# The convolution's running sums in PSUM, and the gate stage's low weight parts on GpSimd

## The reference

```python
h = rmsnorm(x, ln_pre[i])
z = h @ w_in[i]
(c_val, c_glu, c_gate, q, k, v, a_gate, g_conv, g_attn) = split_columns(z)
ya = conformer_conv(c_val, c_glu, w_dw[i], b_dw[i], conv_ln_g[i], conv_ln_b[i], w_pw[i])
ya = (ya * jax.nn.silu(c_gate)) @ w_br_conv[i]
yb = sliding_window_sink_attention(q, k, v, sinks[i], positions)
yb = (yb * jax.nn.silu(a_gate)) @ w_br_attn[i]
m = jax.nn.sigmoid(g_conv) * ya + jax.nn.sigmoid(g_attn) * yb
x = x + rmsnorm(m @ w_out[i], ln_post[i])
x = x + jax.nn.sigmoid(x @ w_ple_gate[i]) * (p[i] @ w_ple_proj[i])
```

## Time and profile before

| | |
|---|---|
| median of 3 runs | 1147.31 us (1146.74 to 1150.53) |
| the profiled execution | 1147.26 us, of which the span from the first to the last instruction is 1145.5 us |
| TensorE busy | 1139.3 us, 99% of the span, 6208 matmuls |
| VectorE busy | 925.0 us, 81%, 1087 instructions |
| ScalarE busy | 421.8 us, 37% |
| GpSimd busy | 29.8 us, 3%, 32 instructions |
| low parts on VectorE (line 1561) | 96 of 1224 ns mean, 117.5 us |
| taps on VectorE (line 1738) | 232, 300.1 us |
| share of TensorE in the chain that ended last | 92% |

### The profile page before, as it was taken

How to read it: one execution, slowest core, us unless ns; L and a number is a source line. 1 busy time by engine, 2 the same in 40 slices (tenths; PEclk the granted TensorE clock), 3 DMA queues, 4 the chain that set the end, 5 groups by cost and what they waited for, 6 DMA issues and landing times.

```text
span 1145.5 us, 16085 instructions
## 1 busy us (share of the span) xinstructions
PE 1139.3 (99%) x6208; PEld 927.8 (81%) x6208; DVE 925.0 (81%) x1087; ACT 421.8 (37%) x763; POOL 29.8 (3%) x32
## 2 busy tenths in 40 slices
PE   9999999999999999999999999999999999999998
PEld 7788888888888888877777788888888888888887
DVE  5999999999999977489888589768767967557776
ACT  6422212212112121266666343332536435444342
POOL 2012010000000000000000000000000000000000
PEclk9999999999999999999999999999999999999999
DMA  9726787421221322411111211346553753334565
GB/s 350 286 92 179 206 238 201 111 92 55 73 86 50 111 51 65 101 38 57 57 57 57 74 49 44 92 135 205 166 173 120 252 182 127 115 117 141 182 200 184
DMA packets 46053, 148.00 MB, mean 129 GB/s; under 512 B 5648, under 2 KB 6416, under 8 KB 43952
## 3 DMA queue, kind: packets, MB, share of 16 engines
q1 hardware_dynamic: 32176, 92.77, 25.5%
q10 hardware_dynamic: 11520, 37.75, 9.5%
q0 software_dynamic: 2304, 16.78, 6.1%
HBM read 119.37 MB, written 41.94 MB: 141 GB/s over the span
## 4 chain that ended last, share of the span: by engine, by line
PE 92%; DMA 3%; DVE 3%; ACT 1%; SPq 1%; issue 1%; DVEq 0%; ACTq 0%
PE psg L629 66%; PE psb L1013 10%; PE psg L921 6%; DMA conv<-xT 2%; PE psb L835 1%; PE psg L892 1%; PE psg L1013 1%; PE psg L682 1%; PE psg L966 1%; PE psg L853 1%; ACT probs L1237 1%; PE psg L887 1%; PE psg L653 1%; PE psg L1037 1%; SPq L496 0%
## 5 line engine op out<-in xcount | busy, mean ns | idle before, releaser
L629 PE MATMUL psg<-h_hi,w_hi 128*128 128x512 f32 x768 | 236.8, 390 | 0.0
L629 PE MATMUL psg<-h_lo,w_hi 128*128 128x512 f32 x768 | 236.5, 389 | 0.0
L629 PE MATMUL psg<-h_hi,w_lo 128*128 128x512 f32 x768 | 236.4, 389 | 0.0
L1561 DVE TENSOR_TENSOR w_lo<-w_raw,w_hi 128x1024 fp32r<-128x1024 f32 x96 | 117.5, 1224 | 86.9 <-ACT w_hi L1093 83.4
L629 PEld LDWEIGHTS psg<-h_hi,w_hi 128*128 128x128 f32 x768 | 143.8, 188 | 30.5 <-issue 0.8
L629 PEld LDWEIGHTS psg<-h_lo,w_hi 128*128 128x128 f32 x768 | 144.1, 188 | 30.0
L629 PEld LDWEIGHTS psg<-h_hi,w_lo 128*128 128x128 f32 x768 | 144.1, 188 | 29.9
L1738 DVE SCALAR_TENSOR_TENSOR conv<-u,cols,conv 128x1024 f32<-128x1024 f32 x120 | 154.3, 1286 | 0.0
L1738 DVE SCALAR_TENSOR_TENSOR work<-u,cols,work 128x1024 f32<-128x1024 f32 x112 | 145.8, 1301 | 0.0
L1093 ACT ACTIVATE w_hi<-w_raw 128x1024 fp32r<-128x1024 f32 x95 | 100.5, 1057 | 103.8 <-PE psg L629 86.4
L1013 PE MATMUL psb<-s_hi,pair_w 128*128 128x512 f32 x240 | 73.9, 389 | 0.0
(11 more groups left out here) (305 smaller groups left out, 1817.5 us busy)
## 6 DMA issues: line engine op xcount, KB each, us to landing
w_raw<-weights SPq DMA_DIRECT2D x97, 512.0 KB, 3.6
gates<-ring ACTq DMA_DIRECT2D x24, 512.0 KB, 2.7
w_sums<-w_pairs POOLq DMA_DIRECT2D x12, 1024.0 KB, 7.8
ring<-gates ACTq DMA_DIRECT2D x24, 512.0 KB, 4.4
block_raw<-w_sums SPq DMA_DIRECT2D x32, 256.0 KB, 3.1
block_raw<-w_pairs SPq DMA_DIRECT2D x24, 256.0 KB, 4.6
x_rows<-x_rows SPq DMA_DIRECT2D x8, 512.0 KB, 10.7
conv<-xT SPq DMA_DIRECT2D x8, 512.0 KB, 14.9
```

Source lines behind the costliest of these rows:

```text
L629: mm = nc.tensor.matmul(psg[:, slot, h * HALF:(h + 1) * HALF], w[:, wslot, (wk + k) * P:(wk + k + 1) * P], r[:, k, h * HALF:(h + 1) * HALF ...
L1561: nc.vector.tensor_tensor(w_lo[:, slot, :], w_raw[:, slot, :], w_hi[:, slot, :].bitcast(F32), ALU.subtract).then_inc(w_lo_ready, 1)
```

## The change

1. The two running sums of the convolution move from SBUF to PSUM: the even one to banks 0 and 1 of `psb` (`conv_banks(0)`), the odd one to banks 2 and 3 (`conv_banks(1)`). The last odd tap (j = 29) writes the result's rows of `conv`, and the closing addition adds the even sum from PSUM to it. The first tap of a block now also waits for the closing addition of the block before.
2. Because banks 2 and 3 are also the place of the transposed values, TensorE waits in `turn_values` for `conv_done` of KT + 1 = 9, the end of all eight convolutions.
3. The low parts of tiles 3 to 33 move from VectorE to GpSimd (`low(t)`): three before the rope tables, two behind them, one behind each of the 16 transfers' issues, the rest at the end. VectorE waits for the last of them and goes on with the low part of tile 34.
4. In the loop over t, VectorE has 8 steps of the convolution in each turn, in place of 7 and 8 by turns.

```diff
--- before.py
+++ after.py
@@ -308,6 +308,10 @@
 
         banks01 = psb[:, 0:2, :].rearrange("p b s -> p (b s)")
 
+        def conv_banks(n):
+
+            return psb[:, 2 * n:2 * n + 2, :].rearrange("p b s -> p (b s)")
+
         def score_banks(jp):
 
             return psb[:, 2 * jp:2 * jp + 2, :].rearrange("p b (h k) -> p (b h) k", h=2)
@@ -792,6 +796,7 @@
                 if k != 1:
                     return
                 pe.wait_ge(ps_free[1], 4 + V_TILE // 2 + 1)
+                pe.wait_ge(conv_done, KT + 1)
                 for c in range(NB):
                     mm = nc.tensor.transpose(psb[:, 2 + c // 4, (c % 4) * P:(c % 4 + 1) * P], v_t[:, c * P:(c + 1) * P], ident[:])
                 mm.then_inc(v_turned, 1)
@@ -1060,21 +1065,37 @@
             pool.wait_ge(w_lo_ready, PLE_STEPS + 1)
             nc.gpsimd.tensor_tensor(w_lo[:, 1, :], w_raw[:, 1, :], w_hi[:, 1, :].bitcast(F32), ALU.subtract).then_inc(w_lo_ready, 1)
 
+            def low(t):
+
+                pool.wait_ge(w_hi_ready, t + PLE_STEPS + 1)
+                pool.wait_ge(w_lo_ready, t + PLE_STEPS)
+                nc.gpsimd.tensor_tensor(w_lo[:, t % 2, :], w_raw[:, t % 2, :], w_hi[:, t % 2, :].bitcast(F32),
+                                        ALU.subtract).then_inc(w_lo_ready, 1)
+
+            low(3)
+            low(4)
+            low(5)
             pool.wait_ge(sin_ready, 1)
             own.step(nc.gpsimd.tensor_tensor(cos_t[:], v_t[:], v_t[:], ALU.mult))
             own.wait()
             nc.gpsimd.tensor_scalar(cos_t[:], cos_t[:], -2.0, 1.0, ALU.mult, ALU.add).then_inc(trig_ready, 1)
             nc.gpsimd.tensor_scalar(sin_t[:], sin_t[:], cols[:, COL_SGN:COL_SGN + 1], None, ALU.mult).then_inc(trig_ready, 1)
-            made = 0
+            low(6)
+            low(7)
+            made, t = 0, 8
             for g in range(2):
-                for t, (copied, added) in ((0, (WPAIR[:, g, 0], 1)), (1, (WSUM[:, g, 0], 3)), (3, (WSUM[:, g, 1], 2)),
+                for n, (copied, added) in ((0, (WPAIR[:, g, 0], 1)), (1, (WSUM[:, g, 0], 3)), (3, (WSUM[:, g, 1], 2)),
                                            (2, (WPAIR[:, g, 1], 3))):
                     if made:
                         pool.wait_ge(sums_made, 16 * made)
-                    pool.dma_start(WSUM[:, g, t], copied).then_inc(sums_made, 16)
+                    pool.dma_start(WSUM[:, g, n], copied).then_inc(sums_made, 16)
+                    low(t)
                     pool.wait_ge(sums_made, 16 * (made + 1))
-                    pool.dma_start(WSUM[:, g, t], WPAIR[:, g, added], accum_op=ALU.add).then_inc(sums_made, 16)
-                    made += 2
+                    pool.dma_start(WSUM[:, g, n], WPAIR[:, g, added], accum_op=ALU.add).then_inc(sums_made, 16)
+                    low(t + 1)
+                    made, t = made + 2, t + 2
+            for n in range(t, Q0):
+                low(n)
             pool.wait_ge(mean_done, 1)
             nc.gpsimd.memset(sums[:], 0.0).then_inc(var_summed, 1)
             rsqrt(3, slice(0, NB // 2))
@@ -1722,23 +1743,25 @@
                     def tap(j):
                         return cols[:, COL_TAPS + i * TAPS + j:COL_TAPS + i * TAPS + j + 1]
 
-                    acc, src = conv[:, i, :], u[i % 2]
+                    acc, more, src = conv_banks(0), conv_banks(1), u[i % 2]
                     dve.wait_ge(ps_free[1], i * 2 + 5)
+                    dve.wait_ge(conv_done, i + 1)
                     own.step(nc.vector.tensor_scalar(acc, src[:, 0:S], tap(0), col("b_dw", i), ALU.mult, ALU.add))
                     yield
                     if i > 0:
                         add_to_mean(i - 1)
                         yield
                     dve.wait_ge(conv_done, i + 1)
-                    own.step(nc.vector.tensor_scalar(work[:], src[:, 1:1 + S], tap(1), None, ALU.mult))
+                    own.step(nc.vector.tensor_scalar(more, src[:, 1:1 + S], tap(1), None, ALU.mult))
                     yield
                     for j in range(2, TAPS):
-                        dst = (acc, work[:])[j % 2]
+                        dst = (acc, more)[j % 2]
                         dve.wait_ge(vec, own.base + own.n - 1)
-                        own.step(stt(dst, src[:, j:j + S], tap(j), dst, ALU.mult, ALU.add))
+                        out = conv[:, i, :] if j == TAPS - 2 else dst
+                        own.step(stt(out, src[:, j:j + S], tap(j), dst, ALU.mult, ALU.add))
                         yield
                     own.wait()
-                    nc.vector.tensor_tensor(acc, acc, work[:], ALU.add).then_inc(conv_done, 1)
+                    nc.vector.tensor_tensor(conv[:, i, :], acc, conv[:, i, :], ALU.add).then_inc(conv_done, 1)
                     yield
                 add_to_mean(KT - 1)
 
@@ -1751,8 +1774,7 @@
             for t in range(2, Q0 - 1):
                 if t % 4 == 2:
                     conv_input(t // 4)
-                tile_low(t + 1)
-                taps(7 if t % 2 == 0 else 8)
+                taps(8)
 
             swap = [p ^ 8 for p in range(32)]
 
@@ -1786,6 +1808,7 @@
                 own.step(nc.vector.tensor_tensor(t[0:ROT], kept[0:ROT], rotated[0:ROT], ALU.add))
                 nc.vector.tensor_tensor(t[HD:HD + ROT], kept[HD:HD + ROT], rotated[HD:HD + ROT], ALU.add).then_inc(last_roped, 1)
 
+            dve.wait_ge(w_lo_ready, PLE_STEPS + Q0)
             tile_low(Q0)
             taps(7)
             for j in range(KT):
```

## The result

| | before | after |
|---|---|---|
| median of 18 runs | 1146.36 us (1145.50 to 1150.53) | 1151.01 us (1148.66 to 1154.77) |
| span of the profiled execution | 1145.5 us | 1148.8 us |
| VectorE busy | 925.0 us | 895.7 us |
| GpSimd busy | 29.8 us | 100.4 us |
| low parts on VectorE / on GpSimd | 96 / 1 | 65 / 32 |

The changed kernel takes 1.0041 times as long as the one before, 95% interval 1.0032 to 1.0049: 4.65 us more. VectorE has 29 us less work, and the kernel is slower all the same, since nobody waited for VectorE.

The account below looks back on a forecast made before the run. TensorE was taken to bound the kernel throughout. 1147.26 us, plus 3.5 for the wait and 1.7 for the clock, gave 1152.5 us, 0.45% more; own range 1151.2 to 1153.8, widened to 1149.8 to 1156.

Parts of the forecast that it names:

- TensorE is the bound: Whole kernel: TensorE sets the time everywhere, so work taken from VectorE can pay nothing by itself.
- One new wait, at the transposes: Inside tile 35: TensorE waits from 414.1 to 417.63 for VectorE's closing addition, 3.5 us.
- The slack of VectorE ahead of the wait: Before the low part of tile 36: taps end at 413.85, VectorE idle until 415.19, cover 1.3 us.
- The clock, 1.7 us between 0 and 3.0: Behind the transposes' wait: clock falls from 2.4 to 1.2 GHz, some 6 us of work at half speed.
- Taps and tensor_scalar in PSUM: VectorE's loop: taps unchanged, bounds -0.02 and +0.05 us each; tensor_scalar at worst 1.29 us, 0.24 us per tile, hidden.
- GpSimd in time: Gate stage: each GpSimd low part, about 2.4 us, is ready before TensorE needs it; no wait.
- The cover of 5.5 us: Worked out at tile 8, for every tile: GpSimd ends at 113.8, TensorE starts the tile at about 119.3.
- A side step: VectorE's taps beside GpSimd: 0.4 us lost per us of GpSimd; all taps hit, 0.95 us more per tile, still fitting.
- rival 3: Gate stage: VectorE shuts GpSimd out, low parts over 7.9 us; 1162 at 8.2 us; chance 0.08 together with another rival.
- rival 1: At the transposes: the wait comes, but the clock stays up or some wait is given back; 1150.3 to 1150.8; chance 0.22.

Follow-up runs that it names:

- turn_at_k4: The changed kernel with the value transposes and their wait behind the fourth k step of tile 35, not the first: 1145.95 us, 0.9995 times before.
- changed_again: The changed kernel itself, unaltered, run once more beside the kernel before: 1151.16 us, 1.0039 times before.
- filled_wait: The changed kernel with the first k step of tile 35 computed twice more ahead of it, 12 matmuls where TensorE waited: 1149.32 us, 1.0024 times before.
- x3_from_tile8: The changed kernel with each of GpSimd's low parts from tile 8 on computed three times: 1151.56 us, 1.0046 times before.
- gpsimd_x3: The changed kernel with each of GpSimd's 31 low parts computed three times: 1157.42 us, 1.0099 times before.
- sums_in_sbuf: The changed kernel with both running sums back in SBUF, low parts still on GpSimd, no TensorE wait for the sums: 1267.93 us median, 1242.42 quickest.
- longer_wait: The changed kernel with five more tensor_scalar on VectorE ahead of the closing addition, results unread: 1156.64 us, 1.0091 times before.
- half_in_psum: The changed kernel with the odd running sum back in SBUF, the even in PSUM, no wait before the transposes: 1147.33 us, 1.0009 times before.

## Why the prediction was right

1. **TensorE is the bound, and less work for VectorE gains nothing.** Right: 29 us less, and 0.9995 of before without the wait (turn_at_k4).
2. **One new wait, at the transposes, 3.5 us.** The transposes came 3.40 us later, and 3.25 us of that were idle in each profile of this order. The chain was the one named: ScalarE's copy of tile 34, the high part of tile 36, its low part, the closing addition. Counted in the time of before (1.42 us later) the addition ended at 417.55, where 417.63 was forecast, and the transposes began at 417.69. At the other end the prediction counted from 414.1, the start of the transposes' weight loads; their matmuls would have begun at 414.29. Both differences are 0.1 to 0.2 us. The slack of VectorE ahead of the wait (1.3 us) was there too: 1.36.
3. **The clock, 1.7 us between 0 and 3.0.** It was 1.35 in the profile after the change, 1.56 and 1.64 in two further ones with the same wait, 2.75 in a fourth, and 1.84 by the medians of changed_again and filled_wait. The granted clock fell 0.5 us before the transposes began in one execution and 1.1 us after it in the next. That there would be a fall, with a price between these bounds, is shown for these traces. But the term isn't one value: the 18 runs of the changed kernel go from no price to speak of (5 of them) to about 5 us (one). The forecast had a middle between bounds, chosen and not derived; that the median came so near is luck.
4. **Taps and tensor_scalar in PSUM.** Taps 1282 ns, inside the bounds. The first tensor_scalar took 1347 ns, above the 1.29 us stated as the worst case, and hidden: 8 x 0.06 us on an engine that waits 20.7 us for TensorE in the stage.
5. **GpSimd in time.** Right for the changed kernel. The cover of 5.5 us was said to hold for every tile. From tile 8 on 4.9 us of it are shown (x3_from_tile8), but not for tiles 3 and 6 (gpsimd_x3); for tile 6 the prediction's own numbers, ready at 92.9 and needed at 97.5, leave 4.6.
6. **A side step that was wrong, though the sum didn't need it.** From the earlier trace rows I took that beside GpSimd it is VectorE that pays, 0.4 us for each us, and that even with all taps hit 10.8 us would fit into a tile of 10.87. The runs show that GpSimd can pay as well, with all of a row of taps: 24.64 us for a low part of 2.4, and 96 to 122 us for the kernel (sums_in_sbuf). Three taps were too few rows for a rate; rival 3 had the mechanism, and the change avoids it by its sums in PSUM.

The prediction calls the stretch from 54.05 on that of tiles 0 to 34; it begins with tile 2. Its 10.87 us for a tile come from counted matmuls and don't hang on that.

As to the level: the three runs that the prediction had of before gave 1147.31 us, all 18, these three among them, 1146.36. In differences the forecast is 5.2 us, the result 4.65; rival 1, the wait without the clock, gave 3.0 to 3.5, and filled_wait measured it at 3.2. The clock is what tells them apart: all four profiles with this wait show it fall. In the five runs in which it stayed at 1.000 rival 1 was right for the execution (3.4 us over before), and the forecast holds for the median.

## What to carry to other kernels

When a change gives a resource to a second user, look for the wait that keeps the two apart, and follow the producer's queue back from it: here the last addition stood behind an instruction that was itself waiting, and the order of these two was worth 2.5 us of waiting and the clock besides. Price a wait of TensorE with the clock behind it: in the traces here it added 1.4 to 2.75 us to a wait of 3.25, and nothing to waits of 0.5 to 1.6. Give it a range, and look at the clock of every run, since one trace shows only one of its values. Before elementwise work goes to GpSimd, look at what VectorE runs beside it: with rows of two-SBUF-input instructions the same 2.4 us of work took up to 29.

## What the runs showed of the hardware

- A wait of 3.25 us brought the granted clock to 0.50 in each of four profiles: for 3.4 us in three (after, changed_again, x3_from_tile8), for over 6 us in one (gpsimd_x3). One of 7.0 us brought it down for 10.3 us (longer_wait), one of 1.9 us for 3.4 us (gpsimd_x3, before tile 6). In 5 of 18 runs of the changed kernel the mean clock was 1.000, so that there it was low for about 1.1 us at most. Waits of 0.53, 0.78 and 1.6 us, with work on both sides, didn't bring it down. The fall came as late as 1.1 us after TensorE had resumed work in changed_again (417.70 against 416.63).
- GpSimd's and VectorE's instructions exclude each other as wholes where VectorE's has two SBUF inputs, in both directions (the tap 2.58 us instead of 1.28, the low part 3.52 instead of 2.40). A tap with one PSUM input isn't affected by a running low part, and both run at full speed (1.28 and 2.40 us, half_in_psum). In rows of taps with two SBUF inputs GpSimd's 2.4 us lasted up to 29.06 us, and at other times of the same execution GpSimd got in between two taps.
- A tensor_scalar of 1024 fp32 columns takes 808 ns from SBUF to SBUF and 1347 to PSUM, so it loses its advantage over a tap; the tap itself loses nothing in PSUM.
